# A hybrid attention block: its compressed branch's first layer as two-part products from the weight ring, another order of projection pieces, an earlier root for two heads

## What is computed

```python
h = rms_norm(x, norm1); proj = h @ w_in
(dq, dk, dv, nq, kc, vc, ksl, vsl, kw, vw, gt) = split(proj)
# 4 differential heads: two softmaxes over 64 dims each, values of 128
a = softmax(q0 k0' / 8 + bias) - lam * softmax(q1 k1' / 8 + bias)
o_diff = rms_norm(a @ v, subln_g) * (1 - lambda_init)
# 8 NSA heads, 2 key/value groups: compressed, selected and window branch
blocks = windows of 32 tokens, stride 16, + pos        # 31 blocks of 32*64 values
kc = gelu(blocks @ w1_k) @ w2_k                        # (31, 2048) @ (2048, 256) @ (256, 64)
vc = gelu(blocks @ w1_v) @ w2_v
o = g0 * o_cmp + g1 * o_slc + g2 * o_win; o_nsa = rms_norm(o, nsa_norm)
x = x + concat(o_diff, o_nsa) @ w_out
x = x + (silu(h2 @ w_gate) * (h2 @ w_up)) @ w_down     # h2 = rms_norm(x, norm2), D_FF 2816
```

## Time and profile before

| | |
|---|---|
| median of 3 runs | 723.78 us (720.46 to 723.93) |
| the profiled execution's own time | 722.78 us |
| its span, first to last instruction | 721.0 us |
| PE busy | 694.7 us, 96% |
| DVE, ACT, POOL busy | 284.5, 287.5, 255.1 us |
| mean granted TensorE clock | 0.981 |
| chain that ended last, PE's share | 60% |

### The profile page before, as it was taken

How to read it: one execution, slowest core, us unless ns; L and a number is a source line. 1 busy time by engine, 2 the same in 40 slices (tenths; PEclk the granted TensorE clock), 3 DMA queues, 4 the chain that set the end, 5 groups by cost and what they waited for, 6 DMA issues and landing times.

```text
span 721.0 us, 9634 instructions
## 1 busy us (share of the span) xinstructions
PE 694.7 (96%) x3559; PEld 579.3 (80%) x3559; DVE 284.5 (39%) x628; ACT 287.5 (40%) x601; POOL 255.1 (35%) x134
## 2 busy tenths in 40 slices
PE   8999999999899978989999999999999999999996
PEld 6988988768798867868878888888888888888884
DVE  4535355343556466543454343342433431003003
ACT  6646355356554247724353223222322331123112
POOL 7632232121122021222265444444444444334422
PEclk9999999999999799989999999999999999999999
DMA  9655240455120121031154233323323332232202
GB/s 249 182 158 150 70 125 9 146 170 167 36 68 10 58 66 30 11 107 36 31 161 124 88 96 109 88 87 104 102 88 89 108 96 88 89 113 91 87 1 116
DMA packets 86413, 68.60 MB, mean 95 GB/s; under 512 B 3060, under 2 KB 75872, under 8 KB 86368
## 3 DMA queue, kind: packets, MB, share of 16 engines
q1 hardware_dynamic: 82616, 63.30, 28.9%
q0 software_dynamic: 1760, 2.52, 1.8%
q10 hardware_dynamic: 1992, 2.17, 1.0%
HBM read 63.77 MB, written 4.47 MB: 95 GB/s over the span
## 4 chain that ended last, share of the span: by engine, by line
PE 60%; DVE 2%; ACT 1%; issue 1%; POOL 0%; DVEq 0%; ACTq 0%; POOLq 0%
PE bank L544 12%; PE bank L545 12%; PE bank L546 12%; PE bank L525 8%; PE bank L527 7%; PE bank L526 7%; PE bank L690 1%; DVE mixT L1130 0%; ACT gate_n L839 0%; PE bank L650 0%; DVE xres L1310 0%; POOL xres L518 0%; PE bank L574 0%; PE bank L666 0%; PE bank L533 0%
## 5 line engine op out<-in xcount | busy, mean ns | idle before, releaser
L498 POOL TENSOR_TENSOR w_lo<-raw,w_hi 128x1024 fp32r<-128x1024 f32 (+1 forms) x96 | 233.1, 2432 | 436.9 <-ACT w_hi L833 436.8
L833 ACT CAST w_hi<-raw 128x1024 fp32r<-128x1024 f32 (+1 forms) x96 | 100.0, 1051 | 226.7 <-PE bank L546 143.9
L544 PE MATMUL bank<-xT_hi,w_hi 128*128 128x512 f32 x464 | 185.1, 399 | 2.6 <-DVE q_diff L1145 2.3
L546 PE MATMUL bank<-xT_hi,w_lo 128*128 128x512 f32 x464 | 183.7, 396 | 0.0
L545 PE MATMUL bank<-xT_lo,w_hi 128*128 128x512 f32 x464 | 183.5, 396 | 0.0
L544 PEld LDWEIGHTS bank<-xT_hi,w_hi 128*128 128x128 f32 x464 | 88.2, 190 | 22.2 <-DVE q_diff L1145 2.5
L546 PEld LDWEIGHTS bank<-xT_hi,w_lo 128*128 128x128 f32 x464 | 88.1, 190 | 19.9
L545 PEld LDWEIGHTS bank<-xT_lo,w_hi 128*128 128x128 f32 x464 | 88.3, 190 | 18.4 <-issue 0.2
L1177 DVE CUSTOM_DVE_ANT_0 bank<-bank,bias 128x128 f32<-128x128 f32 (+3 forms) x96 | 47.7, 498 | 108.4 <-PE bank L651 68.4
L905 ACT ACTIVATE E<-bank,nmax 128x128 f32<-128x128 f32 (+3 forms) x96 | 50.7, 529 | 47.2 <-DVE nmax L1177 45.3
L527 PE MATMUL bank<-w_hi,act_lo 128*128 128x512 f32 x176 | 69.0, 392 | 0.0
(11 more groups left out here) (181 smaller groups left out, 928.4 us busy)
## 6 DMA issues: line engine op xcount, KB each, us to landing
raw<-in_w_gate_dram SPq DMA_DIRECT2D x22, 512.0 KB, 3.8
raw<-in_w_up_dram SPq DMA_DIRECT2D x22, 512.0 KB, 3.7
raw<-in_w_down_dram SPq DMA_DIRECT2D x22, 512.0 KB, 3.8
raw<-in_w_in_dram SPq DMA_DIRECT2D x20, 512.0 KB, 4.4
xres<-in_x_dram SPq DMA_DIRECT2D x8, 512.0 KB, 5.6
raw<-in_w_out_dram SPq DMA_DIRECT2D x8, 512.0 KB, 3.9
bias_rows<-bias_scratch SPq DMA_DIRECT2D x12, 192.0 KB, 4.5
w<-in_cmp_w_k_dram SPq DMA_DIRECT2D x8, 256.0 KB, 4.6
```

The costliest lines, as they stand in the source:

```text
L498: nc.gpsimd.tensor_tensor(wv_lo(k)[:, 0:n], raw[:, k % RAW_SLOTS, 0:n], wv_hi(k)[:, 0:n].bitcast(F32), ALU.subtract).then_inc(s_split, 1)
L544: nc.tensor.matmul(bank[:, :], hi, xT_hi[:, kt, :], start=kt == 0, stop=False)
L546: return nc.tensor.matmul(bank[:, :], lo, xT_hi[:, kt, :], start=False, stop=kt == KT - 1)
L833: nc.scalar.copy(wv_hi(k)[:, 0:n], raw[:, k % RAW_SLOTS, 0:n]).then_inc(s_whi, 1)
```

## The change

Chunks: the eight w1 pieces become chunks of 512 KB, four for each h, of the common ring; `w1`, its semaphores and `load_w1` go. `blk` holds high and low part of the sums side by side (ACT's `block_hi`, DVE's `block_lo`), its float32 form goes to `blk_f`, which lies under k_diff, so dk 1's evacuation waits for it. Each piece of h is four fp32r matmuls of 256 columns, the result's two halves are added by DVE. The cmp merge becomes eight operations that read the bank. The order of jobs and all of `STEP_PIECES` are new: dk before dq, q 2 between the two h, dq 3 before the first mt, og in another order, mt 0 and mt 1 among them. The NSA root moves one step later and takes heads 0 and 1 with it (`EARLY_DIFF`). After the pieces come the first halves of od (0, t), then mt 2 and mt 3, the first halves of od (1, 0) and (1, 1), then the second halves; od uses six banks of its own. Lambda's and four other small loads follow the splits of chunks 5 and 7, and lambda is computed in steps 8 to 10.

```diff
-PROJ_JOBS = [("q", 0), ("k", "ksl"), ("vg", 0), ("vg", 1), ("k", "kw"), ("q", 1),
-             ("dq", 0), ("dk", 0), ("dv", (0, 0)), ("dv", (0, 1)), ("c", 0), ("c", 1), ("q", 2), ("dq", 1), ("h", 0), ("dk", 1),
-             ("h", 1), ("q", 3), ("ht", 0), ("dq", 2), ("hc", 0), ("dk", 2), ("dv", (1, 0)), ("dv", (1, 1)), ("dk", 3),
-             ("mt", 4), ("dq", 3), ("mt", 5), ("mt", 6)]
-OUT_JOBS = [("mt", 7)] + [("og", (z // 4, z % 4)) for z in range(8)]
-OUT_JOBS += [("mt", z) for z in range(4)]
-LAST_JOBS = OUT_JOBS[-6:]
-OUT_JOBS += [("od", (dh, t)) for dh in range(2) for t in range(NT)]
+PROJ_JOBS = [("q", 0), ("k", "ksl"), ("vg", 0), ("vg", 1), ("k", "kw"), ("q", 1), ("dk", 0), ("dq", 0),
+             ("dv", (0, 0)), ("dv", (0, 1)), ("c", 0), ("c", 1), ("dk", 1), ("dq", 1), ("h", 0), ("q", 2),
+             ("h", 1), ("q", 3), ("ht", 0), ("dq", 2), ("hc", 0), ("dk", 2), ("dv", (1, 0)), ("dv", (1, 1)),
+             ("dk", 3), ("dq", 3), ("mt", 6), ("mt", 4), ("mt", 5)]
+OUT_JOBS = [("mt", 7), ("og", (0, 1)), ("og", (0, 3)), ("og", (0, 0)), ("og", (0, 2)), ("mt", 0), ("og", (1, 1)), ("mt", 1),
+            ("og", (1, 2)), ("og", (1, 0)), ("og", (1, 3)), ("mt", 2), ("mt", 3), ("od", (0, 0)), ("od", (0, 1)), ("od", (0, 2)),
+            ("od", (0, 3)), ("od", (1, 0)), ("od", (1, 1)), ("od", (1, 2)), ("od", (1, 3))]
 BASE_JOBS = 4
-STEP_PIECES = (1, 2, 7, 3, 1, 1, 1, 0, 3, 3, 3, 0, 3, 7, 3, 6, 0, 4, 0, 3, 0, 3, 2, 5, 1, 4, 3, 2,
-               1, 0, 6, 0, 2, 3, 3, 2, 0, 1, 1, 2, 2, 2, 0, 4, 4, 0, 0, 1, 8, 1, 0, 1, 0, 0, 5, 0,
-               1, 3, 3, 0, 0, 2, 3, 0, 0, 1, 0, 0, 3, 0, 0, 2, 0, 3, 0, 0, 1, 3, 0, 1, 0, 0, 0, 0,
-               0, 5, 4, 0, 0, 0, 2, 0, 4, 0, 5, 0, 0, 2, 3, 0, 3, 2, 2, 2, 2)
+EARLY_DIFF = 2
+LAMBDA_AFTER = 5
+LAMBDA_STEP = 8
+STEP_PIECES = (3, 1, 3, 5, 1, 1, 1, 1, 0, 5, 5, 1, 3, 2, 12, 0, 3, 1, 2, 2, 0, 1, 3, 1, 4, 2, 1, 4,
+               4, 0, 2, 3, 3, 4, 3, 1, 2, 0, 2, 4, 2, 2, 0, 2, 1, 1, 0, 0, 1, 3, 5, 1, 0, 0, 3, 1,
+               1, 1, 1, 1, 0, 2, 2, 2, 0, 5, 0, 1, 1, 3, 0, 1, 0, 1, 0, 1, 1, 3, 0, 1, 1, 2, 1, 0,
+               4, 0, 0, 1, 0, 1, 1, 0, 4, 0, 3, 0, 2, 3, 1, 2, 3, 2, 2)
...
-    chunks = [j for j in PROJ_JOBS if j[0] not in ("h", "ht", "hc", "mt")]
+    chunks = []
+    for kind, a in PROJ_JOBS:
+        if kind == "h":
+            chunks += [("w1", (a, q)) for q in range(4)]
+        elif kind not in ("ht", "hc", "mt"):
+            chunks.append((kind, a))
...
-            blk = [sb(f"blk{i}", [P, 16, GROUPS, NC], F32, compress) for i in range(2)]
-            w1 = sb("w1", [P, W1_SLOTS, 2 * CMP_HIDDEN], F32, compress)
+            blk = [sb(f"blk{i}", [P, 16, 2, GROUPS * NC], F32R, compress) for i in range(2)]
...
+                blk_f = sb("blk_f", [P, 2, 16 * GROUPS * NC], F32, begin)
...
+                if k == LAMBDA_AFTER:
+                    for n, v in enumerate((lambda_q1, lambda_k1, lambda_q2, lambda_k2)):
+                        pool.dma_start(lam_in[:, n, :], v[0].partition_broadcast(P)).then_inc(s_lamin, 16)
+                if k == LAMBDA_AFTER + 2:
+                    for n, v in enumerate((cmp_w2_k, cmp_w2_v)):
+                        pool.dma_start(w2[:, n, :, :], v[0].rearrange("(m p) d -> p m d", p=P)).then_inc(s_small, 16)
+                    pool.dma_start(cmask[:, :, :], c_cmask).then_inc(s_small, 16)
+                    pool.dma_start(has_cmp[:, :], c_has).then_inc(s_small, 16)
...
+                    kw = index[("w1", (a, piece // 2))]
                     if piece == 0:
-                        pe.wait_ge(s_evac, job_of[("c", a)] + 1)
-                    pe.wait_ge(s_w1raw[n % W1_SLOTS], 16 * (n // W1_SLOTS + 1))
+                        pe.wait_ge(s_blklo, 2 * a + 2)
+                    if piece % 2 == 0:
+                        pe.wait_ge(s_split, kw + 1)
                     for jj in range(2):
-                        mm = nc.tensor.matmul(bank[0:GROUPS * NC, 0:CMP_HIDDEN],
-                                              blk[a][:, 2 * piece + jj, :, :].rearrange("p g n -> p (g n)"),
-                                              w1[:, n % W1_SLOTS, jj * CMP_HIDDEN:(jj + 1) * CMP_HIDDEN],
-                                              start=(piece == 0 and jj == 0), stop=(piece == 7 and jj == 1))
-                    if piece < 7:
+                        c = (2 * (piece % 2) + jj) * CMP_HIDDEN
+                        both = blk[a][:, 2 * piece + jj, :, :].rearrange("p z n -> p (z n)")
+                        o = bank[:, 0:CMP_HIDDEN]
+                        nc.tensor.matmul(o, both, wv_hi(kw)[:, c:c + CMP_HIDDEN], start=piece == 0 and jj == 0, stop=False)
+                        mm = nc.tensor.matmul(o, both, wv_lo(kw)[:, c:c + CMP_HIDDEN], start=False,
+                                              stop=piece == 7 and jj == 1)
+                    if piece % 2 == 1 and piece < 7:
...
+            pe.wait_ge(s_exp, n_slots)
+            pe.wait_ge(s_pt, len(turned))
+            for t in range(NT):
+                for piece in range(2):
+                    proj_piece(job_of[("od", (0, t))], piece)
+            for a in (2, 3):
+                proj_job(job_of[("mt", a)])
+            pe.wait_ge(s_odf, od_upto[-1])
+            pe.wait_ge(s_of, of_upto[-1])
+            for t in range(2):
+                for piece in range(2):
+                    proj_piece(job_of[("od", (1, t))], piece)
+            for dh in range(2):
+                for t in range(NT if dh == 0 else 2):
+                    for piece in range(2, 4):
+                        proj_piece(job_of[("od", (dh, t))], piece)
+            pe.wait_ge(s_evac, job_of[("od", (0, 3))] + 1)
+            for i in range(4):
+                turn_residual(i)
+            for t in range(2, NT):
+                proj_job(job_of[("od", (1, t))])
...
-                if 0 <= was < n_fill:
-                    act.wait_ge(s_job, free_job[was] + 1)
+                if 0 <= was < n_fill and chunks[was][0] == "w1" and chunks[was][1][1] < 3:
+                    act.wait_ge(s_w1, 3 * chunks[was][1][0] + chunks[was][1][1] + 1)
+                elif 0 <= was < n_fill:
+                    act.wait_ge(s_job, freed_by[was][0] + 1)
...
+                if kind == "dk" and a == 1:
+                    act.wait_ge(s_blklo, 4)
...
+            def block_hi(a):
+                act.wait_ge(s_evac, job_of[("c", a)] + 1)
+                nc.scalar.copy(blk[a][:, :, 0, :], blk_sum(a).rearrange("p (l n) -> p l n", l=16)).then_inc(s_blkhi, 1)
...
-                if s == last_nsa + 6:
-                    act.wait_ge(s_ss, 8)
-                    root(16, 20, 512)
+                    square(mix[:, t, 512:1024], mixT[:, 14 + t % 2, :], t, 4 + t)
+                if s == last_nsa + 7:
+                    mixed_root(0, 4 + 4 * EARLY_DIFF, 1)
...
+            def mean_squares(h0, h1):
+
+                a, b = 4 * h0, 4 * h1
+                dve.wait_ge(s_odf, b)
+                link(nc.vector.scalar_tensor_tensor(out=dsum[:, a:b], in0=dsum[:, a:b], scalar=EPS, in1=dsum[:, a:b],
+                                                    op0=ALU.mult, op1=ALU.mult))
+                nc.vector.scalar_tensor_tensor(out=stat[:, 4 + a:4 + b], in0=stat[:, 4 + a:4 + b], scalar=1.0 / P,
+                                               in1=dsum[:, a:b], op0=ALU.mult, op1=ALU.add).then_inc(s_dvar, 1)
...
+                    high, low = (bank[z * GROUPS * NC:(z + 1) * GROUPS * NC, 0:CMP_HIDDEN].rearrange("p (m n) -> p m n", m=2)
+                                 for z in range(2))
+                    z = hid_rows[:, 2 * a:2 * a + 2, :]
+                    link(nc.vector.tensor_copy(z, low))
+                    ins = nc.vector.tensor_tensor(z, high, z, ALU.add)
...
+            def block_lo(a, u):
+
+                if u == 0:
+                    dve.wait_ge(s_blkhi, a + 1)
+                z = slice(8 * u, 8 * u + 8)
+                nc.vector.tensor_tensor(blk[a][:, z, 1, :], blk_sum(a).rearrange("p (l n) -> p l n", l=16)[:, z, :],
+                                        blk[a][:, z, 0, :].bitcast(F32), ALU.subtract).then_inc(s_blklo, 1)
...
-                    z = bank[:, :].rearrange("p (h n) -> p h n", n=HD)
-                    link(nc.vector.tensor_tensor(sq[:, :].rearrange("p (h n) -> p h n", n=HD), z,
-                                                 cstat[:, i, 3, :].unsqueeze(2).to_broadcast([P, NSA_HEADS, HD]), ALU.mult))
-                    c = late_head * HD
-                    nc.vector.tensor_copy(mix[:, i, 512 + c:1024], sq[:, c:512])
-                    m = mix[:, i, 512:512 + c]
-                    nc.vector.tensor_tensor(m, m, sq[:, 0:c], ALU.add).then_inc(s_of, 1)
-                    dve.wait_ge(s_of, of_upto[n])
+                    dve.wait_ge(s_of, of_upto[n] - 1)
+                    for h in range(NSA_HEADS):
+                        z, c = bank[:, h * HD:(h + 1) * HD], cstat[:, i, 3, h:h + 1]
+                        m = mix[:, i, 512 + h * HD:512 + (h + 1) * HD]
```

(20 more changed lines are left out.)

162 lines of the change are left out of this document (80 added, 82 removed).

## The result

The changed kernel takes **700.18 us** (median of four runs, 697.58 to 700.40), the kernel before 723.86; the ratio is 0.967 with the interval 0.963 to 0.971. The forecast was 697.5 with a range of 691 to 709. The profiled execution took 700.08 us, 698.1 of it span, against 722.78 and 721.0 before. The sum of the forecast, -25.6 us, met -22.9 us of span.

A forecast was written before the change was run, and what follows sets the result against it. PE was taken to bound the kernel, so savings before SwiGLU come off the end. Terms -9.0 + 3.0 - 7.1 - 3.5 - 3.5 - 5.5 = -25.6 us gave 697.2 from 722.8, taken as 697.5 us, range 691 to 709.

The forecast's parts named there:

- The first layer, -9.0 and +3.0: Compressed branch, steps 29 to 42: faster matmuls of h save 9.0 us, waits from eight added chunks cost 3 us.
- the two spots that I named: Tightest places for w1's chunks: a split behind dk1's doubling on POOL; ACT waiting 2 to 3 us at step 33.
- The merge, -7.1: Merge of the compressed slots: reading the bank directly removes PE's 2.5 us wait and its lower clock, 7.1 us saved.
- dk 2, -3.5: dk2's first piece moves behind dq2's evacuation: PE's 2.3 us wait and the lower clock after it go, 3.5 us saved.
- waits for exponentials behind casts: Named sign of a wrong forecast: PE waiting for exponentials queued behind casts on ACT.
- dq 3, -3.5: Eight dq3 pieces move into steps 80 to 84 to fill idle PE; half the possible gain taken, 3.5 us saved.
- The end, -5.5: End of attention: mt0 and mt1 run earlier, ending the waits of four transposes and their lower clock, 5.5 us saved.
- the cover that I named: Before mt2 and mt3: eight pieces of od, 5.5 us of PE, needing only mt0 and mt1.
- Middle root and small loads, 0: Earlier scaling of two heads: 0 (-1 to +1.5); small loads and lambda moved: nothing (-1 to +0.5).
- The fourth: Rival: block subtractions and scalings with two SBUF inputs stretch beside POOL, 13 us if all on the path, 710 us; chance 0.04.
- The first rival: ACT and the ring of chunks become the bound: 8 us more than taken, 705 us; chance 0.17.
- the last: Rival: load, cast and split of the added chunks don't overlap, costing 38 us, 732 us; chance 0.03.

The follow-up runs named there:

- e4b: Changed kernel with ACT doing a second cast of every w1 chunk, which POOL then overwrites: 701.44 us, ratio 0.970.
- e2: Changed kernel with POOL's splits of the attention part's chunks cut into four instructions of 256 columns: 694.77 us, ratio 0.960.
- e9: Changed kernel without the 32 matmuls of h by the low parts of the weights: 699.81 us, ratio 0.966.
- e12: Changed kernel without h's 32 low-weight products and without POOL's splits of the eight w1 chunks: 697.33 us, ratio 0.968.
- e1: Kernel before, with only the merge of the compressed slots changed to read from PSUM: 714.76 us, ratio 0.988.
- e6: Changed kernel with the old merge from SBUF put back: 699.59 us, ratio 0.967.
- e8: Kernel before, with the first piece of dk 2 moved from step 51 to step 54: 724.36 us, ratio 1.000.
- e7: Changed kernel with mt 2 and mt 3 put back ahead of the first pieces of od: 700.14 us, ratio 0.966.
- e5: Kernel before, old merge kept, with POOL's splits cut in four: 711.86 us, ratio 0.984.
- e10: Changed kernel with POOL's splits in four, dk 2 moved from step 54 to 55 and og (0, 1) from 92 to 93: 697.77 us, ratio 0.963.
- e3b: Changed kernel with POOL writing zeros three times for each w1 chunk instead of subtracting: 699.17 us, ratio 0.966.

## Why the prediction was right, and where its terms were off

**The bound** was read rightly: PE carries the chain, the second half can't give or take, and the gain comes off the end. PE is busy all of 340 to 690 us, as it was from 354 to 704, and what was saved before was kept.

**The first layer, -9.0 and +3.0.** The pace of 0.12 us was right: the matmuls take 8.0 us where my sum had 7.7. Steps 29 to 42 came out at -2.2 against -3.2, so the "+3.0" measured +4.0. The size was fair, the cause in part another. I put it down to queues on ACT and at the ring. In the kernel after 2.4 of PE's 2.9 us of idle time are waits for DVE, which stands behind POOL's splits, and only 0.4 is the ring; e4b shows that ACT's load isn't it. The ring stands right behind: take DVE's delay away (e2) or work off PE (e9), and PE waits for `w_lo` instead. So the last 3.8 us of the 9 us taken off PE bought nothing. The step that was weak is the average, "POOL 26 of 31.5 us": in the steps of h itself POOL's 2.4 us stand against 1.0 us of PE for a chunk. Of the two spots that I named, the split behind dk 1's doubling shows in e9; ACT waiting for a load shows at 134 us in e12 alone.

**The merge, -7.1,** is -7.6 in steps 68 to 79 of e1; the 3.2 us in steps 80 to 91 I had not counted under it. But it is no term of this sum in the sense in which I wrote it: with the new order it brings about 1 us (e6). I added an edit and an order that both cure one collision.

**dk 2, -3.5,** is the step that failed, on its own: e8 gives 0.0 for it in the kernel before. Removing a wait by moving PE's piece behind it needs somebody else's result to be there sooner; I didn't ask what PE's next instruction would wait for. Steps 43 to 67 missed by 5.9 us through this term and through what my text did not look for there. PE is idle 4.6 us in these steps, 2.7 before: the wait for q_diff fell by 1.3 us only, and new are 1.2 us behind DVE's coefficient at 179.77 us, beside a split, and 2.2 us for exponentials. Of these, 0.9 us comes of DVE, late with a row bound behind another stretched operation (152.59 us, 2.81 long); 0.7 of a load of ACT's function table behind the gelu (1.28 us, at 159.73 us); and 0.6 of a cast (1.04 us, at 166.61). My text had named waits for exponentials behind casts as a sign of being wrong; no run takes them away. The lower clock, 6.8 us in place of 3.4, is the rest, and one execution is too few to put a size on it.

**dq 3, -3.5:** against the merge alone (25.6 us for steps 80 to 91) the kernel after takes 20.7: -4.9, and more than I took. PE is busy all of 243 to 254 us, and the following stretch doesn't suffer, as I had feared for half of it. In steps 68 to 79 1.6 us come back (28.8 against 27.2, with a piece less): PE is idle 1.8 us there, most of it behind the combination at 225.87 us, which takes 2.32 us beside a split and 0.35 alone.

**The end, -5.5:** -6.1 with the moved piece taken out (-5.4 - 0.7), and the cover that I named is hardly needed (e7).

**Middle root and small loads, 0:** start to step 29 gained 1.0 us, 0.4 of it before step 0, and no run isolates them. But this pair of profiles shows the start of the kernel before at its best. In the four profiles with its loads (before, e1, e5, e8) PE waits 0.3, 3.3, 2.6 and 1.6 us for xT_lo near 16 us, and attention begins at 44.8, 48.7, 47.5 and 45.5 us; in two of them 3.4 us at the lower clock are added. In the ten with the new loads (the kernel after and the nine variants of it) the wait is 0.3 us each time, and attention begins at 44.0 to 44.4 us. So moving the small loads and lambda, which I put at nothing, is probably worth some 2 us on average (an estimate, from the means 46.6 and 44.2), and a steadier time.

**The rivals.** The fourth, DVE operations with two SBUF inputs stretched by POOL, was given 0.04 and looked at the wrong instructions. The four new subtractions of blk took 686 ns each on average, near the 0.6 of my text; the attention's coefficients and the combinations of the differential heads, which were there all along, carry the excess of 20.1 us. The Trainium skill (SBUF — State Buffer, Who interferes with whom) says that a VectorE instruction with two SBUF inputs contends with a GpSimd instruction that reads SBUF, not with one that only writes; the splits and the memsets shown above agree with both halves. It also says that the lock is exclusive: whoever issues first has the ports for the whole instruction and the other fully blocks. Here it was longer: at 129.02 us the loser stood to the end of one split and through the whole of the next, 4.41 us where one split takes 2.37. The mistake was to apply the rule to what the change adds, not to every instruction that the changed order puts beside a split. The first rival (0.17) was right in its mechanism for a few steps and wrong in its price, since the ring's waits are 0.4 us in the kernel after; the last, of which "38 us" was to come, measured nothing of the kind, since load, cast and split do overlap. Faster was right, with the terms' errors (+5.9 for steps 43 to 67, +1.0 for 29 to 42, -2.7 for 68 to 91, -1.4 for the rest) partly cancelling: that the sum came within 3 us is in part luck.

**The best version** of these is the changed kernel with POOL's splits in four: 694.8 us.

## What to carry to other kernels

Before pricing an order of work, list for each GpSimd instruction of over a microsecond which VectorE instructions with two SBUF inputs can fall beside it, old ones included, and cut the GpSimd instruction into parts: here that was worth 5 us of 700 in one kernel and 11 in the other. A wait is removed by making its releaser earlier; moving the waiting work later handed the wait to the next instruction in e8, and brought nothing in e10. A stretch at the lower clock that follows a wait in one execution may be missing in the next, so take it from several runs before you count it as a gain. Compare two kernels by a ledger cut at the same steps, and test terms alone in both kernels: two cures for one collision don't add up.

## What the runs showed of the hardware

A VectorE operation on 128x4 values, 0.17 us undisturbed, took 4.41 us beside three splits back to back (POOL's row runs from 126.29 to 133.40, 2.37 us each, so their borders are at 128.7 and 131.0; DVE's operation began at 129.02 and ended at the row's end): it wasn't let in at the border at 131.0. At the next pair of splits it was: the coefficient begun at 135.88 us ended at 138.09, at the border. With splits of a quarter of the length the other such operations fell to 1.2 us and less, but one still stood long:

```profile
136.54 3.53 DVE L1294 SCALAR_TENSOR_TENSOR coef<-dsum,lam,ssum 128x1 f32<-128x1 f32 x1
...
126.16 13.89 POOL L508 TENSOR_TENSOR w_lo<-raw,w_hi 128x256 fp32r<-128x256 f32 x20
```

```profile
L508 POOL TENSOR_TENSOR w_lo<-raw,w_hi 128x256 fp32r<-128x256 f32 x144 | 101.8, 740 | 166.6 <-ACT w_hi L875 166.6
```

It took 3.53 us, the length of five of POOL's parts, inside an unbroken row of twenty (13.89 us, 0.69 each from start to start; the 740 ns of the group overlap a little). So a border between two instructions of POOL lets VectorE in often, not always; what decides it, no run here tells. A cut in four costs POOL 2.8 us a chunk for 2.4.

The same waits of PE, 1.2 us for E and 1.0 to 1.3 for q_diff around 182 us, were followed by 6.8 us at the lower clock in the profile of the kernel after and by none in that of e3b; the steps around them took 57.3 and 55.0 us.
